# Attention matmuls of a hybrid encoder step: every score, turn and value product on the full 128 by 128 array

## The chip, the cores and the metric

The kernel runs on one core of one Trainium2 chip. It uses TensorE (matmuls, with a separate queue for weight loads), VectorE, ScalarE, GpSimd and SyncE, which starts most DMAs. The metric is the device time of one execution in microseconds, as the median of several runs. Before the change that is 2833.0 us (three runs, 2825.91 to 2838.61).

## The reference

Two layers of an encoder run over 512 prompt tokens and 64 sample tokens. Each layer has three sub-layers with a norm before and behind: token mixers, cross-attention into 256 memory tokens, and a squared-ReLU MLP. The mixers are latent attention (8 heads, keys of 64 + 32, values of 64), retention (4 heads), and band attention (8 heads of 64, with a learned bias). The part that matters here is the softmax attention of the two mixers with heads of 64:

```
s = einsum('bqhd,bkhd->bhqk', q, k) * scale (+ bias, or a mask)
p = softmax(s, axis=-1)
o = einsum('bhqk,bkhd->bqhd', p, v)      # v has 64 columns a head
```

The sample tokens attend to 256 cached keys and to their own 64. The memory attention has 4 heads of 128.

## The kernel before

Activations lie feature-major: 128 features on the partitions, all 576 tokens along the free axis. Weights stream in units of 128x1024 and are split into a rounded and a remainder part, so that a projection is three passes of float32r for each of 8 tiles of features, in two halves of 288 tokens (`project`, L332). A projection is called a job; there are two buffers for jobs in PSUM, which VectorE empties.

`attend` runs an attention stage on TensorE, ScalarE and VectorE, each with its own copy of the loop. An item is one head and one tile of 128 queries; there are five a head: four of the prompt, whose keys are the 128, 256, 384 and 512 up to there, and one of the sample tokens, with 320 keys (256 of the cache, 64 new). The scores of an item are issued two items ahead. The order of an item is:

- `scores` (L360): TensorE multiplies queries (stationary) with keys (moving), into one of two banks.
- `maxima` on VectorE: in the band stage first the scaling and the bias (L1024), then the row maximum (L1028).
- `exps` on ScalarE (L697), `normalise` on VectorE (L1036 to L1038).
- `turn` (L370): TensorE transposes the probabilities by tiles of 128 keys, with an identity as the moving operand.
- `copy_turned` on ScalarE (L705, L708): the turned tiles go to SBUF. The last tile of the sample item has 64 keys and gets a copy of its own.
- `weigh` (L381): TensorE multiplies value tiles (stationary) with the turned probabilities. For heads of 64 the stationary operand has 64 columns and the result goes to partitions 0 to 63 or 64 to 127, by the head's parity. For the sample item's third key tile only 64 rows are used.
- `round_output` on ScalarE (L716) and `split_output` on VectorE (L1045), which frees the output bank (`out_free`).

TensorE's order within step j of the loop is: scores of item j+2, weighing of item j-1, turning of item j, and then the projections that a plan puts there for the next head (latent, memory) or the next pair of heads (band). VectorE's order is: normalise item j, the plan's evictions, maxima of item j+2, split of item j-1. `PLAN_MLA` puts keys and values, queries, and the transposed values of the next head behind items of the current one. `PLAN_BAND` puts the projections for queries, keys and values of the next pair, and its values' transposes (L350), behind items 1, 3, 5 and 7 of ten.

In the band stage the queries and keys of a pair of heads share one tile: even head on partitions 0 to 63, odd head on 64 to 127. The scores use 64 rows of both. In the latent stage they use 100 rows (96 features and 4 for the mask). In the memory stage everything is 128 by 128.

`v_sb` holds two buffers of seven value tiles: 0 to 3 prompt, 4 and 5 cache, 6 the new sample tokens. Retention uses the same memory. `cs_sb` holds the cosine and sine tables of latent attention and retention; nothing uses it during the band and memory stages. `Q` is also the scratch for squares (`SQ`) and for retention.

Of the kernel before, what the change touches and what calls it, by code (L numbers as in the profile page):

```python
# [9 lines left out]
ALU = mybir.AluOpType  # L10
ACT = mybir.ActivationFunctionType
AX_X = mybir.AxisListType.X

P = 128
# [9 lines left out]
MASKS = 4  # L24
# [43 lines left out]

Q_TILES = [(i * P, (0, (i + 1) * P), [(j * P, P, j) for j in range(i + 1)]) for i in range(SEQ // P)]
Q_TILES.append((NT - P, (SEQ, DEC + PAST), [(DEC, P, 4), (DEC + P, P, 5), (0, DEC, 6)]))
MEM_TILES = [(i * P, (0, MEM), [(0, P, 0), (P, P, 1)]) for i in range(SEQ // P)]
MEM_TILES.append((NT - P, (MEM, MEM), [(0, P, 2), (P, P, 3)]))
# [52 lines left out]
def build(nc, x_in, mem_in, w_in, ckv_in, kpe_in, state_in, bandk_in, bandv_in, memk_in, memv_in,  # L127
          bias_in, gain_in, gain_x_in, const_in, rope_in, mask_in, y_out, ckv_out, kpe_out, retp_out, rets_out,
          bandk_out, bandv_out, memk_out, memv_out):
    with ExitStack() as ctx:  # L130
# [9 lines left out]
        def tiles(ap, k):  # L140
            return ap.rearrange("p (k n) -> p k n", k=k)
# [24 lines left out]
        TMP, Q, K = tiles(tmp_sb[:, :], 2), tiles(q_sb[:, :], 2), tiles(k_sb[:, :], 2)  # L166
        V = v_sb[:, :].rearrange("p (s t n) -> p s t n", s=2, t=7)
        PROB, BIAS = tiles(prob_sb[:, :], 3), tiles(bias_sb[:, :], 2)
        COS, SIN = cs_sb[:, 0:NT], cs_sb[:, NT:2 * NT]
        SQ = Q  # L170
        SUM = SQ[:, 0]
# [36 lines left out]
        def halves(ap):  # L208
            return ap.rearrange("p (b n) -> p b n", b=2)
# [43 lines left out]
        def _(pe):  # L253
# [15 lines left out]
            with pe.Fori(0, DEPTH) as l:  # L269
# [82 lines left out]

                def scores(i, head):
                    t0, (c, w), _ = head["tiles"][i]
                    r0, r1 = head["rows"]
                    it = n["item"]
                    s = it % 2

                    pe.wait_ge(exp_done, l * ITEMS + it + 1)
                    pe.matmul(score_ps[s][:, 0:w], Q[r0:r1, head["q"], t0:t0 + P], K[r0:r1, head["k"], c:c + w],  # L360
                              start=True, stop=True).then_inc(score_done, 1)
                    n["item"] += 1

                def turn(it, i, head):


                    pe.wait_ge(probs, l * ITEMS + it + 1)
                    pe.wait_ge(turned, l * ITEMS + it + 1)
                    for j, (c, w, _) in enumerate(head["tiles"][i][2]):
                        mm = pe.transpose(turn_ps[0:w, j * P:(j + 1) * P], PROB[:, it % 3, c:c + w], IDENT)  # L370
                    mm.then_inc(turn_done, 1)

                def weigh(it, i, head):

                    kts = head["tiles"][i][2]
                    pe.wait_ge(turned, l * ITEMS + it + 2)

                    pe.wait_ge(out_free, l * ITEMS + it + 1)
                    v0, v1, o0 = head["v"]
                    for j, (c, w, t) in enumerate(kts):  # L380
                        mm = pe.matmul(out_ps[o0:o0 + v1 - v0, 0:P], V[0:w, head["vs"], t, v0:v1],  # L381
                                       probT[0:w, j * P:(j + 1) * P], start=(j == 0), stop=(j == len(kts) - 1))
                    mm.then_inc(out_done, 1)

                def attend(heads, steps, when):
# [52 lines left out]
                def steps_mla(h):  # L438
                    s = []

                    def keys_values():
                        if h == 0:
                            wait_ready()
                        s.append(unit())
                        project(s[0], CR, CKV_HL, at_col=QR * P)
                        project(s[0], CR, CKV_HL, at_col=QR * P, pieces=[(0, PAST, NT)])

                    def queries():
                        if h == 0:
# [5 lines left out]
                    return [keys_values, queries,  # L455
                            lambda: turn_values(V_TOKENS + [(NT, P, 4), (NT + P, P, 5), (SEQ, DEC, 6)], but=1)]

                heads = [dict(q=h % 2, k=h % 2, rows=(0, QK + MASKS), tiles=Q_TILES, vs=h % 2,
                              v=(0, MLA_V, (h % 2) * MLA_V)) for h in range(MLA_HEADS)]
                attend(heads, steps_mla, PLAN_MLA)  # L460
                branch(last_output_split)

# [52 lines left out]

                def steps_band(p):
                    def values():
                        turn_values(V_TOKENS + [(SEQ, DEC, 6)])
                        pe.wait_ge(kv_loaded[p % 2], (l * 4 + p // 2 + 1) * 32)

                    return [lambda: project(unit(), KT, U_HL)] * 3 + [values]

                heads = [dict(q=h // 2 % 2, k=h // 2 % 2, rows=((h % 2) * 64, (h % 2) * 64 + 64),
                              tiles=Q_TILES, vs=h // 2 % 2, v=((h % 2) * 64, (h % 2) * 64 + 64, (h % 2) * 64))
                         for h in range(BAND_HEADS)]
                attend(heads, steps_band, PLAN_BAND)

# [12 lines left out]
                def steps_mem(h):  # L540
                    def query():
# [6 lines left out]
                heads = [dict(q=h % 2, k=h % 2, rows=(0, P), tiles=MEM_TILES, vs=h % 2, v=(0, P, 0))  # L548
                         for h in range(MEM_HEADS)]

                for step in steps_mem(0)[:MEM_FIRST]:
# [52 lines left out]
        def _(act):  # L604
# [40 lines left out]
            with act.Fori(0, DEPTH) as l:  # L645
# [55 lines left out]
                def copy_turned(it, i, head):  # L701
                    kts = head["tiles"][i][2]
                    act.wait_ge(turn_done, l * ITEMS + it + 1)
                    full = sum(k[1] == P for k in kts)
                    ins = act.activation(probT[:, 0:full * P], turn_ps[:, 0:full * P], ACT.Copy)  # L705
                    if full < len(kts):
                        w = kts[-1][1]
                        ins = act.activation(probT[0:w, full * P:(full + 1) * P],  # L708
                                             turn_ps[0:w, full * P:(full + 1) * P], ACT.Copy)
                    ins.then_inc(turned, 1)  # L710

                def round_output(it, i, head):
                    t0, t1, c0 = out_tokens(head["tiles"], i)
# [176 lines left out]
        def _(dve):  # L890
# [19 lines left out]
            with dve.Fori(0, DEPTH) as l:  # L910
# [9 lines left out]
                def free(ins):  # L920
                    ins.then_inc(job_free, 1)
# [199 lines left out]
                def steps_mla(h):  # L1121
# [27 lines left out]

                    def values():  # L1150
                        s = job()
                        v.tensor_copy(V[:, b, 0:4, 0:MLA_V], tiles(job_ps[s][:, 0:512], 4)[:, :, NOPE:P])
                        v.tensor_copy(V[:, b, 4:6, 0:MLA_V], tiles(job_ps[s][:, 512:768], 2)[:, :, NOPE:P])
                        free(v.tensor_copy(V[0:DEC, b, 6, 0:MLA_V], job_ps[s][0:DEC, 768 + NOPE:768 + P]))

                    return [keys_values, queries, values]

# [539 lines left out]
```

## Time and profile before

| | |
|---|---|
| median of the runs | 2833.0 us |
| profiled execution | 2829.17 us |
| its span | 2827.4 us, 46601 instructions |
| TensorE busy | 2606.2 us (92%), weight loads 2395.7 us (85%) |
| VectorE, ScalarE, GpSimd busy | 1443.0 (51%), 799.8 (28%), 826.7 (29%) |
| chain that ended last | TensorE 79%, VectorE 10%, its sequencer 6% |
| mean granted clock of TensorE | 0.959 |

The chain that ended last is followed back from the last instruction, at each step to what released it or to the instruction before it on its engine. A matmul's end is modelled and overlaps the next one's start, so the distance between starts tells what a pass costs, not its length. The latent stages run from 86.8 to 211.5 us in the first layer and from 1480.8 to 1605.6 in the second (first scores to last weighing), the band stages from 531.9 to 684.6 and from 1929.7 to 2080.2, the memory stages from 861.1 to 924.9 and from 2255.4 to 2321.7.

### The profile page before, as it was taken

Reading aid. Unit: us, or ns where it says so; the run is one execution under the profiler, and the core shown is the slowest. Engines: PE = TensorE matmul, PEld = TensorE weight load, DVE = VectorE, ACT = ScalarE, POOL = GpSimd, SP = SyncE. Lnnn points to the kernel's source line nnn. Section 1 sums busy time; section 2 is a strip of 40 time slices with the busy share of each in tenths; the row PEclk is TensorE's granted clock in tenths of the full one; section 3 lists DMA queues with packets and bytes.
Section 4 is the critical chain, followed back from the end, with each engine's and each line's share of the span. In section 5 each row is a group of like instructions: output and inputs, shape, how many; then the busy total and the mean of one; then the engine's idle time right before and its main releaser. Section 6 shows DMA issues by size and latency. Waiting matters only on the chain.

```text
span 2827.4 us, 46601 instructions
## 1 busy us (share of the span) xinstructions
PE 2606.2 (92%) x17836; PEld 2395.7 (85%) x17836; DVE 1443.0 (51%) x2226; ACT 799.8 (28%) x1460; POOL 826.7 (29%) x335
## 2 busy tenths in 40 slices
PE   8789999999989799999788999899999898999996
PEld 7669888877988799999676798797779787999995
DVE  4661464354564755346756515624445648353366
ACT  4342112234324311111324421223343343111112
POOL 3113223211333234434221132132223232343342
PEclk9999999999999999999899999899999999999998
DMA  4102112221223122222221121121222221222222
GB/s 140 38 23 93 60 47 85 71 75 61 83 71 94 46 82 84 88 82 84 61 82 31 48 83 49 43 92 61 81 76 80 68 89 48 83 85 83 82 83 78
DMA packets 65687, 204.73 MB, mean 72 GB/s; under 512 B 7936, under 2 KB 16000, under 8 KB 65360
## 3 DMA queue, kind: packets, MB, share of 16 engines
q10 hardware_dynamic: 47808, 174.08, 20.1%
q1 hardware_dynamic: 17680, 27.90, 3.0%
q8 instruction: 136, 2.23, 0.3%
q14 instruction: 63, 0.52, 0.1%
HBM read 190.93 MB, written 11.03 MB: 71 GB/s over the span
## 4 chain that ended last, share of the span: by engine, by line
PE 79%; DVE 10%; DVEq 6%; issue 2%; ACT 1%; DMA 0%; SPq 0%; ACTq 0%
PE job L332 65%; PE outp L381 5%; PE scores L360 3%; DVE rstd L974 3%; PE turn L370 2%; DVEq L1001 2%; PE scores L262 1%; DVEq L1037 1%; PE job L341 1%; DVE arena L965 1%; DVE rstd L982 1%; PE job L350 1%; ACT probT L705 1%; DVE x L1002 1%; DVEq L980 0%
## 5 line engine op out<-in xcount | busy, mean ns | idle before, releaser
L332 PE MATMUL job<-arena,w_hi 128*128 128x288 f32 (+1 forms) x9984 | 1775.5, 300 | 46.5 <-DVE q L1139 16.7
L332 PEld LDWEIGHTS job<-arena,w_hi 128*128 128x128 f32 x9984 | 1494.3, 192 | 67.6 <-issue 22.3
L593 POOL TENSOR_TENSOR w_lo<-raw,w_hi 128x1024 fp32r<-128x1024 f32 x331 | 826.5, 2497 | 1968.7 <-ACT w_hi L612 1968.7
L332 PE MATMUL job<-arena,w_lo 128*128 128x288 f32 (+1 forms) x4992 | 1087.6, 297 | 0.0
L332 PEld LDWEIGHTS job<-arena,w_lo 128*128 128x128 f32 x4992 | 818.8, 191 | 0.0
L612 ACT ACTIVATE w_hi<-raw 128x1024 fp32r<-128x1024 f32 x331 | 349.6, 1056 | 1072.0 <-PE job L332 904.7
L381 PEld LDWEIGHTS outp<-probT,v 128*64 128x64 f32 (+2 forms) x992 | 111.4, 149 | 141.5 <-issue 71.3
L948 DVE TENSOR_TENSOR tmp<-job,rstd 128x576 f32<-128x576 f32 x70 | 53.0, 758 | 329.9 <-PE job L332 325.5
L381 PE MATMUL outp<-probT,v 128*64 128x128 f32 (+2 forms) x992 | 160.8, 291 | 51.4 <-DVE arena L1045 38.7
L262 PE MATMUL scores<-q,const 128*128 128x288 f32 (+1 forms) x296 | 99.0, 473 | 69.6 <-ACT q L673 60.6
L360 PE MATMUL scores<-k,q 128*128 128x256 f32 (+10 forms) x400 | 148.5, 455 | 13.1 <-DVE k L1341 4.4
L937 DVE CAST arena<-tmp 128x576 fp32r<-128x576 f32 x64 | 151.6, 2368 | 4.7
L716 ACT ACTIVATE arena<-outp 64x128 fp32r<-64x128 f32 (+3 forms) x200 | 52.4, 262 | 312.9 <-PE outp L381 312.5
L262 PEld LDWEIGHTS scores<-q,const 128*128 128x128 f32 x296 | 60.8, 222 | 92.1 <-ACT q L673 69.2
L1387 DVE TENSOR_TENSOR m<-job,m 128x576 f32<-128x576 f32 x48 | 36.4, 758 | 194.3 <-PE job L332 194.3
L747 ACT ACTIVATE tmp<-tmp,gain 128x576 f32<-128x576 f32 x48 | 37.3, 778 | 256.4 <-DVE tmp L948 256.4
L1376 DVE SCALAR_TENSOR_TENSOR tmp<-job,rstd 128x576 f32<-128x576 f32 x64 | 48.5, 758 | 110.4 <-PE job L332 110.1
L943 DVE COPY m<-job 128x576 f32<-128x576 f32 x48 | 36.3, 756 | 124.9 <-PE job L332 124.9
L370 PE MATMUL turn<-const,prob 128*128 128x128 f32 (+1 forms) x496 | 99.7, 300 | 0.0
L974 DVE RECIPROCAL rstd<-rstd 128x576 f32<-128x576 f32 x22 | 82.5, 3752 | 31.3 <-ACT rstd L626 27.4
L705 ACT ACTIVATE probT<-turn 128x256 f32<-128x256 f32 (+3 forms) x200 | 83.6, 418 | 36.4 <-PE turn L370 32.3
L1045 DVE TENSOR_TENSOR arena<-outp,arena 64x128 fp32r<-64x128 f32 (+3 forms) x200 | 55.0, 275 | 65.3 <-ACT arena L716 60.8
(145 smaller groups left out, 1718.1 us busy)
## 6 DMA issues: line engine op xcount, KB each, us to landing
raw<-in_w ACTq DMA_DIRECT2D x332, 512.0 KB, 3.6
bias<-in_bias SPq DMA_DIRECT2D x16, 256.0 KB, 3.4
x<-in_x SPq DMA_DIRECT2D x4, 576.0 KB, 8.7
cs<-in_rope SPq DMA_DIRECT2D x4, 576.0 KB, 4.6
out_o_bandk<-k SPq DMA_DIRECT2D x8, 288.0 KB, 4.0
out_o_bandv<-tmp SPq DMA_DIRECT2D x8, 288.0 KB, 5.0
out_y<-x SPq DMA_DIRECT2D x1, 2304.0 KB, 6.9
bias<-in_mem SPq DMA_DIRECT2D x8, 256.0 KB, 3.5
```

The source lines that it names most:

```text
L262: mm = pe.matmul(scores_ps[:, po:po + nn], ONES, SQ[:, k % 2, so:so + nn], start=(k == 0), stop=(k == kt - 1))
L332: mm = pe.matmul(ps[0:m, po:po + nn], w[:, s, c:c + m], x[:, k, so:so + nn], start=(k == 0 and w is WHI and x is hl[0]), stop=(k == kt - 1 ...
L360: pe.matmul(score_ps[s][:, 0:w], Q[r0:r1, head["q"], t0:t0 + P], K[r0:r1, head["k"], c:c + w], start=True, stop=True).then_inc(score_done, 1)
L370: mm = pe.transpose(turn_ps[0:w, j * P:(j + 1) * P], PROB[:, it % 3, c:c + w], IDENT)
L381: mm = pe.matmul(out_ps[o0:o0 + v1 - v0, 0:P], V[0:w, head["vs"], t, v0:v1], probT[0:w, j * P:(j + 1) * P], start=(j == 0), stop=(j == len ...
L593: nc.gpsimd.tensor_tensor(WLO[:, u % RING, :], RAWS[:, u % RAW, :], WHI[:, u % RING, :].bitcast(F32), ALU.subtract).then_inc(lo_done, 1)
L612: act.activation(WHI[:, u % RING, :], RAWS[:, u % RAW, :], ACT.Copy).then_inc(hi_done, 1)
L705: ins = act.activation(probT[:, 0:full * P], turn_ps[:, 0:full * P], ACT.Copy)
L937: v.tensor_copy(hi, src)
L974: v.reciprocal(ap, ap)
L1001: dve.drain()
L1045: v.tensor_tensor(O_HL[1][o0:o1, ot, t0:t1], out_ps[o0:o1, c0:P], O_HL[0][o0:o1, ot, t0:t1].bitcast(F32), ALU.subtract).then_inc(out_free, 1)
```

## The change

- The weighing takes value tiles 128 columns wide. The result has 128 rows, of which a head of 64 uses the same 64 as before. In the latent stage the values of an even head lie in columns 0 to 63, of an odd head in columns 64 to 127, and the other columns hold whatever is there; in the band stage a tile holds both heads of a pair, as it did.
- Band queries get two tiles, one for even and one for odd heads, with zeros in the other head's 64 partitions. The scores multiply over all 128 rows. The even tile is `Q`, the odd one lies in `cs_sb`. VectorE scales the query projection in two operations, one for each, and sets the zeros once a layer, before the retention branch's output.
- The 64-long tail tile becomes 128 long: its transposes and its product cover 128 keys, where the probabilities of the extra 64 are multiplied with value rows that are zero. ScalarE copies all turned tiles in one instruction.
- At the start VectorE sets `v_sb` and `vT` to zero.

```diff
-Q_TILES = [(i * P, (0, (i + 1) * P), [(j * P, P, j) for j in range(i + 1)]) for i in range(SEQ // P)]
-Q_TILES.append((NT - P, (SEQ, DEC + PAST), [(DEC, P, 4), (DEC + P, P, 5), (0, DEC, 6)]))
+Q_TILES = [(i * P, (0, (i + 1) * P), [(j * P, j) for j in range(i + 1)]) for i in range(SEQ // P)]
+Q_TILES.append((NT - P, (SEQ, DEC + PAST), [(DEC, 4), (DEC + P, 5), (0, 6)]))
...
+        Q_EVEN, Q_ODD = Q, tiles(cs_sb[:, :], 2)
...  (scores, turn, weigh on TensorE)
-                    pe.matmul(score_ps[s][:, 0:w], Q[r0:r1, head["q"], t0:t0 + P], K[r0:r1, head["k"], c:c + w],
+                    pe.matmul(score_ps[s][:, 0:w], head["q"][0:rows, t0:t0 + P], K[0:rows, head["k"], c:c + w],
...
-                    for j, (c, w, _) in enumerate(head["tiles"][i][2]):
-                        mm = pe.transpose(turn_ps[0:w, j * P:(j + 1) * P], PROB[:, it % 3, c:c + w], IDENT)
+                    for j, (c, _) in enumerate(head["tiles"][i][2]):
+                        mm = pe.transpose(turn_ps[:, j * P:(j + 1) * P], PROB[:, it % 3, c:c + P], IDENT)
...
-                    v0, v1, o0 = head["v"]
-                    for j, (c, w, t) in enumerate(kts):
-                        mm = pe.matmul(out_ps[o0:o0 + v1 - v0, 0:P], V[0:w, head["vs"], t, v0:v1],
-                                       probT[0:w, j * P:(j + 1) * P], start=(j == 0), stop=(j == len(kts) - 1))
+                    for j, (_, t) in enumerate(kts):
+                        mm = pe.matmul(out_ps[:, 0:P], V[:, head["vs"], t, :], probT[:, j * P:(j + 1) * P],
+                                       start=(j == 0), stop=(j == len(kts) - 1))
...
-                heads = [dict(q=h // 2 % 2, k=h // 2 % 2, rows=((h % 2) * 64, (h % 2) * 64 + 64),
-                              tiles=Q_TILES, vs=h // 2 % 2, v=((h % 2) * 64, (h % 2) * 64 + 64, (h % 2) * 64))
+                heads = [dict(q=(Q_EVEN, Q_ODD)[h % 2][:, h // 2 % 2], k=h // 2 % 2, rows=P, tiles=Q_TILES, vs=h // 2 % 2)
...  (copy_turned on ScalarE)
-                    full = sum(k[1] == P for k in kts)
-                    ins = act.activation(probT[:, 0:full * P], turn_ps[:, 0:full * P], ACT.Copy)
-                    if full < len(kts):
-                        w = kts[-1][1]
-                        ins = act.activation(probT[0:w, full * P:(full + 1) * P],
-                                             turn_ps[0:w, full * P:(full + 1) * P], ACT.Copy)
-                    ins.then_inc(turned, 1)
+                    w = len(kts) * P
+                    act.activation(probT[:, 0:w], turn_ps[:, 0:w], ACT.Copy).then_inc(turned, 1)
...  (VectorE)
             v.memset(small[:, :], 0.0)
+            v.memset(v_sb[:, :], 0.0)
+            v.memset(vT, 0.0)
...
-                        v.tensor_copy(V[:, b, 0:4, 0:MLA_V], tiles(job_ps[s][:, 0:512], 4)[:, :, NOPE:P])
+                        o = b * MLA_V
+                        v.tensor_copy(V[:, b, 0:4, o:o + MLA_V], tiles(job_ps[s][:, 0:512], 4)[:, :, NOPE:P])
...
                 dve.sem_inc(phase_done, 1)
+                for b in range(2):
+                    v.memset(Q_EVEN[BAND_HD:P, b], 0.0)
+                    v.memset(Q_ODD[0:BAND_HD, b], 0.0)
                 branch(False, ahead=1)
...
+                    def queries():
+
+                        s = job()
+                        e = BAND_HD
+                        v.tensor_tensor(halves(Q_EVEN[0:e, b]), job_halves(s, 0, e), halves(rstd[0:e, :]), ALU.mult)
+                        free(v.tensor_tensor(halves(Q_ODD[e:P, b]), job_halves(s, e, P), halves(rstd[e:P, :]), ALU.mult))
...
-                    return [lambda: scale_job(Q[:, b]), keys, lambda: scale_job(vT[:, 0:NT]), values]
+                    return [queries, keys, lambda: scale_job(vT[:, 0:NT]), values]
```

## Rows read from the trace of the kernel before

**Rows 1.** Groups by shape, L381: count | busy us, mean ns | idle before
```profile
L381 PE MATMUL outp<-probT,v 128*64 128x128 f32 x768 | 122.4, 291 | 44.5 <-DVE arena L1045 33.1 <-ACT probT L705 8.4 <-ACT probT L708 2.5
...
L381 PE MATMUL outp<-probT,v 64*64 64x128 f32 x64 | 14.2, 304 | 0.0
```

**Rows 2.** Timeline, TensorE, latent stage: start us, us, engine, line, operation
```profile
156.37 1.02 PE L360 MATMUL scores<-k,q 100*128 100x512 f32 x2
157.32 0.43 PE L381 MATMUL outp<-probT,v 128*64 128x128 f32 x2
157.69 0.44 PE L370 MATMUL turn<-const,prob 128*128 128x128 f32 x2
157.96 0.70 PE L360 MATMUL scores<-k,q 100*128 100x320 f32 x2
```

**Rows 3.** Timeline, TensorE, memory stage
```profile
893.19 0.60 PE L360 MATMUL scores<-k,q 128*128 128x256 f32 x2
893.63 0.61 PE L381 MATMUL outp<-probT,v 128*128 128x128 f32 x4
894.07 0.38 PE L370 MATMUL turn<-const,prob 128*128 128x128 f32 x2
894.29 0.38 PE L350 MATMUL job<-const,tmp 128*128 128x128 f32 x2
...
895.02 0.68 PE L381 MATMUL outp<-probT,v 128*128 128x128 f32 x4
895.54 0.38 PE L370 MATMUL turn<-const,prob 128*128 128x128 f32 x2
```

**Rows 4.** Chain that ended last, one latent head: start us, us, what
```profile
140.68 0.75 DVE q L1134
...
144.22 0.62 PE outp L381 x4
...
147.78 0.60 ACT probT L705
...
154.15 0.13 PE job L332
```

**Rows 5.** Windows of two latent heads each: length, busy by engine, PEclk, DMA
```profile
122.43:154.15 31.72, 28.32 (x186) 21.61 (x186) 22.34 (x61) 14.37 (x44) 4.72 (x2) 1.00 0.12 34
154.15:188.99 34.84, 31.44 (x186) 24.34 (x186) 22.31 (x61) 14.37 (x44) 4.73 (x2) 0.90 0.11 31
```

**Rows 6.** Chain that ended last, one band pair
```profile
581.54 6.39 PE job L332 x48
...
602.29 0.13 PE job L332
```

**Rows 7.** Timeline, TensorE, band stage
```profile
576.18 1.06 PE L381 MATMUL outp<-probT,v 128*64 128x128 f32 x8 [0.93 <-DVE arena L1045]
...
579.69 1.12 PE L360 MATMUL scores<-k,q 64*128 64x512 f32 x2
580.74 0.43 PE L381 MATMUL outp<-probT,v 128*64 128x128 f32 x2
...
590.30 0.87 PE L381 MATMUL outp<-probT,v 128*64 128x128 f32 x6 [0.17 <-ACT probT L705]
```

**Rows 8.** Timeline, VectorE, band stage
```profile
580.31 0.35 DVE L1038 TENSOR_SCALAR prob<-prob,small 128x256 f32<-128x256 f32 x1
...
587.97 0.76 DVE L948 TENSOR_TENSOR q<-job,rstd 128x576 f32<-128x576 f32 x1 [4.92 <-PE job L332]
```

**Rows 9.** Timeline, VectorE, latent stage: a copy of 64 partitions
```profile
151.62 0.75 DVE L1144 COPY k<-job 64x576 f32<-64x576 f32 x1 [0.90 <-PE job L332]
```

**Rows 10.** Line 1169, a memset: count, ns min/median/max, first and last start
```profile
L1169 DVE MEMSET v<- x2: 165/165/165, 289.8 to 1683.9; 64x128 f32 x2
```

**Rows 11.** Timeline, end of the retention branch, first layer
```profile
446.31 0.76 DVE L948 TENSOR_TENSOR tmp<-job,rstd 128x576 f32<-128x576 f32 x1 [2.10 <-DMA out_o_rets<-k]
...
449.07 0.69 PE L332 MATMUL job<-arena,w_hi 128*128 128x288 f32 x4
```

More of the change, by code:

```diff
@@ L66 @@
 NCONST = _c
-Q_TILES = [(i * P, (0, (i + 1) * P), [(j * P, P, j) for j in range(i + 1)]) for i in range(SEQ // P)]
-Q_TILES.append((NT - P, (SEQ, DEC + PAST), [(DEC, P, 4), (DEC + P, P, 5), (0, DEC, 6)]))
-MEM_TILES = [(i * P, (0, MEM), [(0, P, 0), (P, P, 1)]) for i in range(SEQ // P)]
-MEM_TILES.append((NT - P, (MEM, MEM), [(0, P, 2), (P, P, 3)]))
+Q_TILES = [(i * P, (0, (i + 1) * P), [(j * P, j) for j in range(i + 1)]) for i in range(SEQ // P)]
+Q_TILES.append((NT - P, (SEQ, DEC + PAST), [(DEC, 4), (DEC + P, 5), (0, 6)]))
+MEM_TILES = [(i * P, (0, MEM), [(0, 0), (P, 1)]) for i in range(SEQ // P)]
+MEM_TILES.append((NT - P, (MEM, MEM), [(0, 2), (P, 3)]))
 NQ = len(Q_TILES)
@@ L354, in scores @@
                     t0, (c, w), _ = head["tiles"][i]
-                    r0, r1 = head["rows"]
+                    rows = head["rows"]
                     it = n["item"]
@@ L455, in steps_mla @@
                     return [keys_values, queries,
-                            lambda: turn_values(V_TOKENS + [(NT, P, 4), (NT + P, P, 5), (SEQ, DEC, 6)], but=1)]
-                heads = [dict(q=h % 2, k=h % 2, rows=(0, QK + MASKS), tiles=Q_TILES, vs=h % 2,
-                              v=(0, MLA_V, (h % 2) * MLA_V)) for h in range(MLA_HEADS)]
+                            lambda: turn_values(V_TOKENS + [(NT, P, 4), (NT + P, P, 5), (SEQ, P, 6)], but=1)]
+                heads = [dict(q=Q[:, h % 2], k=h % 2, rows=QK + MASKS, tiles=Q_TILES, vs=h % 2) for h in range(MLA_HEADS)]
                 attend(heads, steps_mla, PLAN_MLA)
@@ L517, in values @@
                     def values():
-                        turn_values(V_TOKENS + [(SEQ, DEC, 6)])
+                        turn_values(V_TOKENS + [(SEQ, P, 6)])
                         pe.wait_ge(kv_loaded[p % 2], (l * 4 + p // 2 + 1) * 32)
                     return [lambda: project(unit(), KT, U_HL)] * 3 + [values]
-                heads = [dict(q=h // 2 % 2, k=h // 2 % 2, rows=((h % 2) * 64, (h % 2) * 64 + 64),
-                              tiles=Q_TILES, vs=h // 2 % 2, v=((h % 2) * 64, (h % 2) * 64 + 64, (h % 2) * 64))
+                heads = [dict(q=(Q_EVEN, Q_ODD)[h % 2][:, h // 2 % 2], k=h // 2 % 2, rows=P, tiles=Q_TILES, vs=h // 2 % 2)
                          for h in range(BAND_HEADS)]
@@ L546, in steps_mem @@
                         lambda: turn_values([(0, P, 0), (P, P, 1)]), query]
-                heads = [dict(q=h % 2, k=h % 2, rows=(0, P), tiles=MEM_TILES, vs=h % 2, v=(0, P, 0))
+                heads = [dict(q=Q[:, h % 2], k=h % 2, rows=P, tiles=MEM_TILES, vs=h % 2)
                          for h in range(MEM_HEADS)]
@@ L1151, in values @@
                         s = job()
-                        v.tensor_copy(V[:, b, 0:4, 0:MLA_V], tiles(job_ps[s][:, 0:512], 4)[:, :, NOPE:P])
-                        v.tensor_copy(V[:, b, 4:6, 0:MLA_V], tiles(job_ps[s][:, 512:768], 2)[:, :, NOPE:P])
-                        free(v.tensor_copy(V[0:DEC, b, 6, 0:MLA_V], job_ps[s][0:DEC, 768 + NOPE:768 + P]))
+                        o = b * MLA_V
+                        v.tensor_copy(V[:, b, 0:4, o:o + MLA_V], tiles(job_ps[s][:, 0:512], 4)[:, :, NOPE:P])
+                        v.tensor_copy(V[:, b, 4:6, o:o + MLA_V], tiles(job_ps[s][:, 512:768], 2)[:, :, NOPE:P])
+                        free(v.tensor_copy(V[0:DEC, b, 6, o:o + MLA_V], job_ps[s][0:DEC, 768 + NOPE:768 + P]))
                     return [keys_values, queries, values]
```

## The prediction

> **What bounds the kernel now.** I read the page first: TensorE is busy for 92% of the 2827.4 us span and the chain that ended last is 79% TensorE, so time is mostly a matter of what TensorE issues and how densely. The diff touches three kinds of TensorE work, the scores (L360), the turning of probabilities (L370) and the weighing of values (L381), in the two stages of 8 heads (latent, then band). Of the weighing's passes 768 run as 128 rows by 64 columns, and 64 more as 64 by 64 (a float32 product is two passes) [rows 1]. Then I read TensorE's timeline where nothing waits, in the latent stage, beside the memory stage, whose heads are 128 wide and whose code the change leaves alone. There the difference stands in the starts. In the memory stage four weighing passes take 0.44 us from their first start to the first turn (893.63 to 894.07), 0.11 each, and two turns 0.22 (to 894.29) [rows 3]. In the latent stage two weighing passes take 0.37 to the first turn (157.32 to 157.69), and two turns then 0.27 (to 157.96) [rows 2]. So entering and leaving the narrow shape costs something that the full shape doesn't.
>
> **Price of one crossing.** Scores of 256 columns take 0.22 a pass (0.44 for two, 893.19 to 893.63) [rows 3]; 512 columns would take 0.43, two 0.86. In the latent stage two such passes take 0.95 before the weighing starts [rows 2]: 0.09 for going in. Two weighing passes would take 0.22 and take 0.37: 0.15 for the slower first step (about 0.05) and for going out (0.09). The first step after it, among the turns, has 0.27 for 0.22: 0.05. A crossing is 0.09 before and 0.05 behind; I count 0.145, since the rows are rounded to 0.01 and the two together gave 0.15 above. In the band stage scores read 64 rows: 512 columns take 1.05 [rows 7] where the latent stage has 0.95, so going into scores costs 0.09 + 0.10 = 0.19.
>
> The Trainium skill (TensorEngine Tiling (Array Packing), Key Properties) says that changing the tiling mode, not just the tile, drains TensorE. The 0.09 agrees with it in kind; the page gives no time. By its letter every matmul on part of the array would count, and the turns of 64 columns with them; my sum counts only crossings that cost something in the starts.
>
> **What goes, and what it is worth where.** All crossings: latent 80 items with one in, one out, and 16 more for the 64-long tail tile, 176 x 0.145 = 25.5 us; band 160 x 0.145 + 80 x 0.19 + 16 x 0.145 = 40.7 us. 66 us is the most, if TensorE set every step. It doesn't, so I go by stretches of one period.
>
> *Latent head, 15.86 us* (31.72 for two) [rows 5]. From 140.68 the chain is VectorE's (queries of the next head, the next maximum, the split of the last output), until the weighing may start at 144.22 [rows 4]. Crossings in that stretch are hidden and stay worth nothing. From 144.22 to 154.15 the chain is TensorE's but for ScalarE's copy of 0.60 (147.78). On it lie six crossings: into the weighing of 6 passes, out of it, out of the one of 8, into the one of 4 + 2, within it (128 to 64 rows), out of it: 0.87. Added: a weighing that starts out of a wait shows its load. In the memory stage four passes out of a wait take 0.52 (895.02 to 895.54) against 0.44 without one [rows 3], 0.08. A load of half the columns shows part of that already; between 0 and 0.08 I take 0.06, nearer to the row, for the weighing of 8, and 0.02 for passes a few ns longer. 0.79 a head. ScalarE's and VectorE's pieces in that stretch have over 0.3 us to spare before the step that needs them, so the next limit is not reached. Seven heads a layer carry this; the last has no projections in between, its weighings wait for ScalarE, and the tail's second copy goes: about 1.0. (7 x 0.79 + 1.0) x 2 layers = 13.0 us.
>
> *Band pair, about 40.7 us*, four stretches between its three projections.
> - After the value projection VectorE sets the pace (bias, maximum, normalising, copying values) to 576.18, where TensorE had waited 0.93 for its split [rows 7]; only the start of that line comes earlier, by 0.19 (shorter scores). +0.19.
> - 576.18 to 581.54 [rows 6, 7] holds eight crossings, 1.25 us, all on TensorE's chain. But VectorE is nearly as late: it normalised what the last turn needs until 580.66 [rows 8], and its work ahead of that stands without a gap, so it moves by 0.03 at most. The turn can start 0.05 behind it, at 580.68 instead of 581.10 (the 0.37 that two weighing passes take from 580.74, [rows 7, 2]): +0.42 of the 1.25.
> - Behind the query projection the change adds work: queries are scaled into two tiles. Now it is one operation of 0.76 at 587.97 [rows 8]; each of the two has 64 partitions and the same 576 columns, and a copy of 64x576 took 0.75 [rows 9]. Bounds: nothing (halves of 0.38) to 0.76 more; I take 0.72, by the copy and the overlap of neighbours. Queued behind it on VectorE are bias, maximum and split, which the weighing at 590.30 waits for; that weighing waited 0.17 for ScalarE already [rows 7]. It would start near 590.87, the next projection 0.46 later after what the crossings give back. -0.46.
> - Behind the key projection, to 602.29 [rows 6], seven crossings, 1.1 us; VectorE has slack, ScalarE's copy holds back 0.2. +0.89.
>
> 1.04 a pair, three pairs a layer; the last pair, without projections, half VectorE's, about 1.3; the prelude 0.3. (3.1 + 1.3 + 0.3) x 2 = 9.4 us.
>
> *Added elsewhere.* Four memsets of 64x576 a layer, on VectorE before the retention branch's output. A memset of 64x128 took 0.165 us [rows 10]; four cost 0.7 at least (no part of it by length) and 3.0 at most (all of it); I take 2.2, since most of such a price goes by length. Behind them waits the scaling at 446.31, which frees the buffer that TensorE takes at 449.07 [rows 11]: 446.31 + 2.2 + 0.76 = 449.27, 0.2 late here; I count the other layer at nothing, its spare time being of the same kind. Bounds 0 to 3.0 a layer; I take 0.2 in all. The two memsets at the start (2624 columns, 2 to 3.4 us by the same row) run while inputs are loading: nothing. The latent values' copies keep their sizes; the tail tile's longer turn and product cost no pass.
>
> *Sum*: 13.0 + 9.4 - 0.2 = 22 us. The profiled execution took 2829.2; it becomes 2807. The median of the runs lies 3.8 higher (2833.0), so I predict 2811.
>
> **Rivals**, their times against the runs' median.
> 1. *VectorE takes the place of the drains* in the latent stage too, and the band stage gives only its fourth stretches: half of the latent 13.0 and 5 of the band's 9.4 are left, 11 or 12. 2821. For it: VectorE is already the chain in three of the band's stretches. Against: in 144.22 to 154.15 no VectorE piece stands on the chain.
> 2. *The clock.* Two latent heads had a granted clock of 0.90 on average instead of 1.00 (parts of them at 1.2 in place of 2.4 GHz) and took 34.84 instead of 31.72 [rows 5], 1.56 each. TensorE's waits in VectorE's stretches get longer by what the crossings lose there. If nine more latent heads fell so, 14 us go back: 2825, no change that can be told. Against: what TensorE has to stream is the same or more.
> 3. *Slower: the full-width load.* 832 passes [rows 1] load 128 columns in place of 64. Exposed, it costs 0.06 (above); at every pass, on the chain, 832 x 0.06 = 50 us: 2833 - 22 + 50 = 2861. It decides from about 370 exposed loads on the chain on (22 / 0.06), and below that only eats the gain. Against: inside a row of passes the full shape keeps 0.11 [rows 3], so the load lies under the pass before; only starts out of a wait show it. The Trainium skill (TensorE: Matmul & The Clock Gate, LDWEIGHTS) has the load's time grow with the columns, P/1.2 ns, so about 53 ns more; by it, uncovered, 832 x 0.053 = 44 us would be added. The starts out of a wait agree with that size, the streams show it covered.
> 4. *It doesn't do what it says*: the 0.09 comes of the kind of work (product, then turn), not of its shape. Then only the added work is left, 0.2 for the memsets and 0.46 for the queries of three pairs in two layers: 2836. Against: the memory stage has the same order and no 0.09 [rows 3].
>
> **How the numbers follow.** Forecast 0.69, rival 1 0.12, rival 2 0.10, rival 3 0.05, rival 4 0.04. 0.5% (14 us) is about what a measurement of this kernel can tell from no change; faster by more means under 2819. That is the forecast but for its upper edge (0.65), and a part of the case of VectorE (0.05): 0.70. Same 0.25, slower 0.05 (the load alone). The range of 8 in 10: low end 2796, if VectorE's lines in the band stage give way and 37 of the 66 us come back; high end 2829, with the clock case and rival 1.
>
> **What would show it.** The weighing has one form, 128 by 128, and no idle time put down to issue; two weighing passes to the turn 0.22; latent heads near 15.1 us, band pairs near 39.7; latent stages shorter by 6 to 7 us, band stages by 4 to 5; VectorE the chain from 576 to 581. Wrong: a 0.09 that stays between weighing and turns, stages that keep their length, latent heads with a granted clock under 1 in most periods, or time lost outside the two stages.

## The result, and the profile after

| | before | after |
|---|---|---|
| median of 20 runs each | 2830.5 us (2812.2 to 2839.4) | 2810.1 us (2797.8 to 2827.2) |
| ratio after / before | | 0.9931, 95% interval 0.9914 to 0.9947 |
| profiled execution | 2829.17 us, span 2827.4 | 2799.22 us, span 2797.4 |
| mean granted clock | 0.959 | 0.963 |
| latent stage, layers 1 and 2 | 124.67, 124.76 | 123.35, 118.90 |
| of it at half clock (1.2 GHz) | 10.2, 10.2 | 20.5, 10.2 |
| band stage | 152.74, 150.45 | 144.42, 144.24 |
| of it at half clock | 18.7, 11.4 | 6.8, 6.8 |

About 20 us less, 0.7%. The page of the kernel after (busy time by engine; the chain by engine; the weighing's group):

```profile
PE 2556.0 (91%) x17836; PEld 2407.1 (86%) x17836; DVE 1453.8 (52%) x2244; ACT 799.2 (29%) x1428; POOL 827.6 (30%) x335
...
PE 77%; DVE 11%; DVEq 7%; issue 3%; ACT 1%; DMA 0%; SPq 0%; ACTq 0%
...
L381 PE MATMUL outp<-probT,v 128*128 128x128 f32 x992 | 157.8, 291 | 71.8 <-DVE arena L1040 59.9
```

The two narrow groups of [rows 1] have become one, 128 by 128, with as many passes as all forms had together. Most of its idle time stands beside VectorE (L1040, the split of the last output, 59.9 of 71.8 us), as it did before (33.1 of 44.5 in the larger narrow group). So a crossing doesn't show as idle time, before or after; it shows in the starts, below. The chain has less of TensorE and more of VectorE.

TensorE's timeline in the latent stage of the kernel after, where nothing waits (start us, length, engine and line, operation):

```profile
158.22 1.02 PE L361 MATMUL scores<-k,q 100*128 100x512 f32 x2
159.08 0.38 PE L381 MATMUL outp<-probT,v 128*128 128x128 f32 x2
159.30 0.38 PE L371 MATMUL turn<-const,prob 128*128 128x128 f32 x2
159.52 0.70 PE L361 MATMUL scores<-k,q 100*128 100x320 f32 x2
```

This answers to [rows 2]. Two weighing passes to the turn take 0.22 where they took 0.37, the two turns 0.22 for 0.27, the scores 0.86 for 0.95. These are the steps of the memory stage in [rows 3].

The same view at the weighing that VectorE holds back, in the kernel after and then before:

```profile
126.12 0.70 PE L361 MATMUL scores<-k,q 100*128 100x320 f32 x2
128.55 0.68 PE L381 MATMUL outp<-probT,v 128*128 128x128 f32 x4 [1.73 <-DVE arena L1040]
```

```profile
144.22 0.62 PE L381 MATMUL outp<-probT,v 128*64 128x128 f32 x4 [1.45 <-DVE arena L1045]
```

The wait has grown from 1.45 to 1.73 us. What the crossings lost in VectorE's stretch (0.29 in the steps above), TensorE now spends waiting. Two heads of the kernel after as windows (length, then busy time and count of TensorE, its loads, VectorE, ScalarE and GpSimd, granted clock, DMA share, GB/s):

```profile
109.72:124.82 15.10, 13.10 (x95) 11.36 (x93) 11.52 (x30) 7.27 (x21) 2.36 (x1) 1.00 0.11 36
124.82:141.44 16.62, 14.64 (x94) 13.01 (x93) 10.72 (x30) 7.09 (x21) 2.36 (x1) 0.90 0.11 33
```

At full clock a pair of neighbouring heads takes 14.97 + 15.10 us, where two took 31.72 in [rows 5]. A head with a stretch at half clock takes 16.6 to 16.8.

The chain of the kernel after through one band pair (start, length, what; "DVEq" is VectorE's sequencer):

```profile
573.34 0.39 DVE prob L1033
573.72 0.46 DVEq L1021
...
577.71 0.44 PE turn L371 x2
578.15 6.40 PE job L333 x48
...
584.58 0.75 DVE q L1306
585.33 0.78 DVEq L1021
...
587.59 0.91 PE outp L381 x6
...
588.93 6.38 PE job L333 x48
595.31 0.43 PE scores L361 x2
...
598.59 1.47 PE job L333 x11
```

From 573.34 on VectorE is the chain up to the last two turns (577.71). That stretch, 573.21 to 578.15, takes 4.94 where it took 5.36. Behind the query projection (584.55) two VectorE pieces of about 0.75 stand in the chain (584.58, and 585.33, the second scaling, shown as its sequencer), and 4.38 us pass to the next projection instead of 3.83. Behind the key projection nothing but TensorE is left: 3.28 (595.31 to 598.59) instead of 4.15. TensorE's timeline of that pair:

```profile
573.21 1.13 PE L381 MATMUL outp<-probT,v 128*128 128x128 f32 x8 [1.20 <-DVE arena L1040]
574.17 0.49 PE L371 MATMUL turn<-const,prob 128*128 128x128 f32 x3
...
576.12 1.02 PE L361 MATMUL scores<-k,q 128*128 128x512 f32 x2
577.18 0.46 PE L381 MATMUL outp<-probT,v 128*128 128x128 f32 x2
...
587.59 0.91 PE L381 MATMUL outp<-probT,v 128*128 128x128 f32 x6 [1.51 <-DVE arena L1040]
```

Scores of 512 columns take 1.06 to the weighing (576.12 to 577.18), but that weighing is one that VectorE is late for: its split ends at 577.03. The 8 passes at 573.21 take 0.96 from a wait to the turn.

### The profile page after: what moved, and what is told of

It is laid out like the page before. It is cut to its first block, busy times and chain, and to the rows that moved or that the text cites. A ratio compares the mean times of both kernels' runs of the same rounds, so it can differ in the third digit from the quotient of the medians.

```text
span 2797.4 us, 46587 instructions
## 1 busy us (share of the span) xinstructions
PE 2556.0 (91%) x17836; PEld 2407.1 (86%) x17836; DVE 1453.8 (52%) x2244; ACT 799.2 (29%) x1428; POOL 827.6 (30%) x335
## 4 chain that ended last, share of the span: by engine, by line
PE 77%; DVE 11%; DVEq 7%; issue 3%; ACT 1%; DMA 0%; SPq 0%; ACTq 0%
PE job L333 65%; PE outp L381 4%; DVE rstd L969 3%; PE scores L361 2%; DVEq L996 2%; DVEq L1032 2%; PE turn L371 1%; PE scores L263 1%; PE job L342 1%; DVE arena L960 1%; PE job L351 1%; DVE rstd L977 1%; DVE prob L1019 1%; DVEq L1021 1%; ACT probT L703 1%
## 5 line engine op out<-in xcount | busy, mean ns | idle before, releaser
L333 PE MATMUL job<-arena,w_hi 128*128 128x288 f32 (+1 forms) x9984 | 1770.6, 299 | 47.6 <-DVE q L1134 16.8
L381 PEld LDWEIGHTS outp<-probT,v 128*128 128x128 f32 x992 | 135.2, 196 | 139.3 <-ACT probT L703 75.7
L381 PE MATMUL outp<-probT,v 128*128 128x128 f32 x992 | 157.8, 291 | 71.8 <-DVE arena L1040 59.9
L361 PE MATMUL scores<-k,q 128*128 128x256 f32 (+9 forms) x320 | 115.9, 449 | 12.1 <-DVE k L1347 4.4
L371 PE MATMUL turn<-const,prob 128*128 128x128 f32 x496 | 91.6, 283 | 1.0 <-DVE prob L1033 0.6
L1033 DVE TENSOR_SCALAR prob<-prob,small 128x256 f32<-128x256 f32 (+4 forms) x200 | 76.0, 380 | 17.1 <-issue 1.8
```

What stands on the lines that cost most here:

```text
L333: mm = pe.matmul(ps[0:m, po:po + nn], w[:, s, c:c + m], x[:, k, so:so + nn], start=(k == 0 and w is WHI and x is hl[0]), stop=(k == kt - 1 ...
L361: pe.matmul(score_ps[s][:, 0:w], head["q"][0:rows, t0:t0 + P], K[0:rows, head["k"], c:c + w], start=True, stop=True).then_inc(score_done, 1)
L371: mm = pe.transpose(turn_ps[:, j * P:(j + 1) * P], PROB[:, it % 3, c:c + P], IDENT)
L381: mm = pe.matmul(out_ps[:, 0:P], V[:, head["vs"], t, :], probT[:, j * P:(j + 1) * P], start=(j == 0), stop=(j == len(kts) - 1))
L1033: v.tensor_scalar(PROB[:, it % 3, 0:w], PROB[:, it % 3, 0:w], small[:, s * 4 + 3:s * 4 + 4], None, ALU.mult).then_inc(probs, 1)
```

## The experiments

A pair is one period of the band stage, at full clock and with the next pair's projections in it. "Low heads" counts the latent periods (one head to the next), of 14 in a profile, with more than 1 us at half clock. The last kernel has a single execution and no ratio.

| kernel | ratio to before (95%) | pair, us | full-clock latent heads, us | low heads |
|---|---|---|---|---|
| before | 1 | 40.66 | 15.83, 15.89 | 5 |
| after | 0.9931 (0.9914 to 0.9947) | 39.73 | 14.97, 15.10 | 7 |
| after, repeated | 0.9928 (0.9903 to 0.9953) | 39.73 | 14.97, 15.12 | 8 |
| narrow values in the memory stage of before | 1.0005 (0.998 to 1.003) | 40.65 | 15.85, 15.88 | 3 |
| after, band scores on 64 rows | 0.9966 (0.9948 to 0.9985) | 39.78 | 14.98, 15.09 | 7 |
| before, band scores on 128 rows | 0.9971 (0.9953 to 0.9989) | 40.44 | 15.83, 15.89 | 2 |
| after, second scaling deferred | 0.9940 (0.9918 to 0.9962) | 38.81 | 14.97, 15.09 | 9 |
| the same, repeated | 0.9929 (0.9903 to 0.9955) | 38.83 | 14.98, 15.10 | 9 |
| and band values copied by ScalarE | 0.9895 (0.9871 to 0.9920) | 37.90 | 14.97, 15.12 | 8 |
| after, filled wait | 0.9887 (0.9860 to 0.9913) | 39.74 | 14.98, 15.11 | 0 |
| all three | **0.9845 (0.9823 to 0.9868)** | 37.91 | 14.98, 15.11 | 0 |
| before, later queries (one run) | | 40.66 | 16.20, 16.25 | 7 |

### Narrow values in the memory stage

The shape alone, in a stage that the change leaves alone. Half of the memory heads' output is left out.

```diff
-heads = [dict(q=h % 2, k=h % 2, rows=(0, P), tiles=MEM_TILES, vs=h % 2, v=(0, P, 0))
+heads = [dict(q=h % 2, k=h % 2, rows=(0, P), tiles=MEM_TILES, vs=h % 2, v=(0, 64, 0))
```

> The kernel before, but the memory attention, which was 128 by 128, weighs only 64 of its 128 value columns (the other half of its output is left out). Theory (the shape's change costs, 0.09 us before and 0.05 behind each crossing): four weighing passes to the first turn take 0.58 us instead of 0.44, two turns then 0.27 instead of 0.22, scores to weighing 0.09 more; 40 items gain two crossings each, 11.6 us at most, about 6 on the chain; the memory stages get longer by 2 to 5 us each, nothing else changes. Rival (the cost comes of the order product then turn, or of waits, not of the shape): 0.44 and 0.22 stay and the memory stages keep their length.

TensorE's timeline in its memory stage:

```profile
897.91 0.60 PE L360 MATMUL scores<-k,q 128*128 128x256 f32 x2
898.43 0.65 PE L381 MATMUL outp<-probT,v 128*64 128x128 f32 x4
899.01 0.44 PE L370 MATMUL turn<-const,prob 128*128 128x128 f32 x2
899.29 0.38 PE L350 MATMUL job<-const,tmp 128*128 128x128 f32 x2
899.51 0.60 PE L360 MATMUL scores<-k,q 128*128 128x256 f32 x2
```

The 64-column passes bring with them what [rows 2] has: scores to weighing 0.52 instead of 0.44 in [rows 3], four passes to the turn 0.58 instead of 0.44, the turns 0.28 instead of 0.22. A head takes 19.51 us instead of 18.98. So the price belongs to the shape, not to the kind of work; rival 4 falls. In total 8 heads lose 0.53 each, which no ratio of this kernel can show, and it doesn't. The Trainium skill (TensorEngine Tiling (Array Packing), Key Properties) says that a change of tiling mode drains TensorE. The trace agrees for the products, not for the turns of 64 columns that the kernel before had, each of which starts 0.11 us behind the turn before it, like a full one.

### Band scores on 64 rows again

```diff
-heads = [dict(q=(Q_EVEN, Q_ODD)[h % 2][:, h // 2 % 2], k=h // 2 % 2, rows=P, ...
+heads = [dict(q=Q[:, h // 2 % 2], k=h // 2 % 2, rows=(h % 2 * 64, h % 2 * 64 + 64), ...
...  (VectorE: the zeros go too)
-    return [queries, keys, lambda: scale_job(vT[:, 0:NT]), values]
+    return [lambda: scale_job(Q[:, b]), keys, lambda: scale_job(vT[:, 0:NT]), values]
```

> The changed kernel with the band scores put back on 64 rows: one query tile, one scaling, no zeros set for it; weighing, turns and tail stay full. Theory (each stretch goes by what sets it, TensorE or VectorE): latent heads stay at 15.06 us. A band pair: behind the value projection +0.19, the stretch that VectorE sets 0 to +0.1, behind the query projection -0.73 (the second scaling goes), behind the key projection +0.62 (two crossings into scores at 0.19, two out of them at 0.145): +0.2 a pair, 39.9 instead of 39.7, 1 to 2 us for the program over the changed kernel. Rival (every crossing counts in full): 80 x (0.19 + 0.145) less 6 x 0.75, 22 us over the changed kernel, so as slow as before.

TensorE's timeline in its band stage:

```profile
575.52 1.12 PE L361 MATMUL scores<-k,q 64*128 64x512 f32 x2
576.57 0.49 PE L381 MATMUL outp<-probT,v 128*128 128x128 f32 x2
```

1.05 for two passes of 512 columns on 64 rows, as in [rows 7], and the pair is as long as with the padding: 39.78 against 39.73. The zero-padded queries, as they stand, buy nothing in a pair; what they save in crossings, the second scaling spends. The ratio is nearer to 1 than that of the kernel after (0.9966 against 0.9931, about 10 us); no part of the pairs explains that. The band stages, 145.49 and 146.67 us against 144.94 in the mean of four with the padding, hold 2 us of it; the rest stays open.

### Band scores on 128 rows alone

The reverse: the kernel before with the two query tiles and `rows=(0, P)` in the band stage, values and tail tile as they were.

> The kernel before with the band scores alone padded to 128 rows (two query tiles, two scalings, zeros set once a layer); weighing and tail stay narrow. Theory: latent heads stay at 15.87 us. A band pair: behind the value projection -0.19, next stretch -0.38, behind the query projection +0.65, behind the key projection -0.38: -0.3, 40.4 instead of 40.66; the program 2 us under the kernel before, not to be told from it. Rival (the padding carries the gain of the band stage): pairs near 39.7, band stages 5 us shorter each.

Pairs of 40.44, as expected, and latent heads as before. The pairs' 0.22 times 6 explain 1.3 us of the 8 that the ratio gives (0.0029 of 2833). The band stages, 146.88 and 148.80 us against 150.96 in the mean of four with 64-row scores, are 6 us shorter together, so the padding takes more off the stage than off its pairs: half clock was 6.8 and 11.4 us there, 13.2 in the mean of the four. And this profile has little half clock in its latent stages (2 low heads against 5), so its ratio says less of the edit than its pairs.

### The second scaling deferred

The odd queries' scaling moves into the step of the next job, ahead of the keys' scaling, where VectorE waits for the key projection and has time to spare.

```diff
 def queries():
     ...
-    free(v.tensor_tensor(halves(Q_ODD[e:P, b]), job_halves(s, e, P), halves(rstd[e:P, :]), ALU.mult))
 def keys():
+    s = (n["job"] - 1) % 2
+    e = BAND_HD
+    free(v.tensor_tensor(halves(Q_ODD[e:P, b]), job_halves(s, e, P), halves(rstd[e:P, :]), ALU.mult))
```

> The changed kernel, but VectorE scales the odd heads' queries one step later, in the time in which it waits for the key projection; the same operations. Theory (the second scaling stands on the chain only because bias, maximum and split are queued behind it): the stretch behind the query projection falls from 4.38 to about 3.63 us, pairs from 39.7 to 39.0, 6 pairs: 4.5 us under the changed kernel, ratio to the kernel before about 0.9915. Rival (the stretch is set by ScalarE's copy or by the turns anyway): 4.38 falls by 0.2 at most and the pairs stay at 39.6.

The chain behind its query projection:

```profile
583.32 0.75 DVE q L1306
584.07 0.13 DVEq L1021
...
585.43 0.91 PE outp L381 x6
...
586.77 6.38 PE job L333 x48
```

One scaling in the chain, and 3.47 us from the projection's end (583.30) to the next one (586.77) instead of 4.38. The pair falls by 0.92 to 38.81. The whole 0.76 of the second scaling had been on the path, and a little more. But the ratio didn't tell this kernel from the kernel after. Both were run again, side by side:

> The changed kernel once more, beside the next two on the same chip. Theory: ratio to the kernel before 0.993 again; latent heads 15.06 us where the granted clock is full, band pairs 39.7 and 40.1. The feed-forward stages, which the change leaves alone, run at one of two paces of a pass, 130.0 or 133.3 ns, whichever kernel it is; 10 us a stage.

> The kernel with the odd heads' queries scaled one step later, once more. Theory: pairs of 38.8 and 39.2 us, so 5.5 us under the changed kernel where the feed-forward stages run at the same paces; the timed ratio 0.991 to 0.994. Rival (what the band pairs give back goes elsewhere, as the first timing, 0.994, may say): the stages outside the band stage get longer by as much.

The pairs repeat to 0.03 us, and the ratios still don't part (0.9928 and 0.9929). 0.92 x 6 is 5.5 us, and the intervals are 14 us wide; but the traces show where the 5.5 went. The end of the first band stage as windows, from the weighing behind the last scores of 512 columns to the last weighing, in the kernel after and then with the scaling deferred:

```profile
666.90:675.95 9.05, 5.87 (x41) 4.54 (x40) 5.59 (x16) 4.81 (x14) 0.00 (x0) 1.00 0.00 0
663.81:675.51 11.70, 8.53 (x40) 6.87 (x39) 5.58 (x16) 4.81 (x14) 0.00 (x0) 0.70 0.00 0
```

VectorE and ScalarE do the same work in both, but TensorE's granted clock is 0.70, and the stretch is 2.65 us longer. All four band stages of the two deferred profiles end so, and one of four in the kernel after. The deferred stages take 144.31 to 144.56 us, as long as the three of the kernel after that end at full clock (144.22 to 144.42). So the rival of the repetition is right in that what the pairs give back goes elsewhere: into the last head of the same stage. TensorE's waits there are the same in both (1.0, 0.69 and 0.58 us), so why its clock falls in one of them stays open.

### The band values copied by ScalarE

Beside the deferred scaling, ScalarE takes the two copies of the band values out of PSUM.

```diff
 def values():    # ScalarE
+    n["job"] += 1
+    act.wait_ge(job_done, l * JOBS + n["job"] + 1)
+    s = (n["job"] - 1) % 2
+    act.activation(V[:, p % 2, 0:4, :], tiles(job_ps[s][:, 0:512], 4), ACT.Copy)
+    act.activation(V[0:DEC, p % 2, 6, :], job_ps[s][0:DEC, 768:768 + P], ACT.Copy).then_inc(job_free, 1)
...
 def values():    # VectorE
-    s = job()
-    v.tensor_copy(V[:, b, 0:4, :], tiles(job_ps[s][:, 0:512], 4))
-    free(v.tensor_copy(V[0:DEC, b, 6, :], job_ps[s][0:DEC, 768:768 + P]))
+    n["job"] += 1
```

> As the kernel with the deferred queries, and ScalarE instead of VectorE copies the band values out of PSUM (0.69 + 0.27 us a pair). Theory (VectorE sets the stretch behind the value projection): 0.9 us less a pair, pairs near 38.0 and 38.3, 10 to 11 us under the changed kernel at equal paces, ratio 0.989. Rival (TensorE or ScalarE is next within 0.3 us there): pairs near 38.5 and 38.9.

ScalarE's timeline in its band stage (the copies stand ahead of the exponentials of the sample item):

```profile
571.02 0.60 ACT L817 ACTIVATE v<-job 128x512 f32<-128x512 f32 x1
571.52 0.26 ACT L818 ACTIVATE v<-job 64x128 f32<-64x128 f32 x1
```

Pairs of 37.90, another 0.91 less. With VectorE in three of the four stretches, what is taken from it shows at once. The band stages take 138.80 and 139.06 us, 5.5 less than with the deferred scaling alone: half of that is the pairs', the other half comes from the last head, which here stays at full clock.

### The wait filled

In the profiles with narrow latent values 10 of 42 latent periods were low (the expectation below says 9 and four kernels; it was 10 and three), in those with wide ones 48 of 84. Inside the heads, each fall came within 1.5 us behind the wait for VectorE's query work. So four passes are put there whose result is overwritten before it is read.

```diff
...  (in the latent stage's call: fill=True)
+if fill and j % NQ == 2 and j + NQ < len(flat):
+    pe.wait_ge(job_free, l * JOBS + at["job"] + n["job"] + 1)
+    for _ in range(2):
+        pe.matmul(job_ps[n["job"] % 2][:, 0:3 * P], IDENT, const[:, 0:3 * P], start=True, stop=True)
 if j:
     weigh(base + j - 1, flat[j - 1][1], flat[j - 1][0])
```

> The kernel after, with two products of the identity and 384 constant columns (four passes, about 1.3 us, overwritten before anything reads them) put on TensorE in the latent stage of heads 0 to 6, in front of the weighing that waits for VectorE's query work. In the profiles of the four kernels with narrow latent values, 9 of 42 latent head periods had a stretch at half clock; in those of the six profiles with wide ones, 48 of 84. What stands ahead of each is the same wait of TensorE, 1.44 us in the narrow form and 1.73 in the wide one. Theory (the longer wait brings the clock down): the wait falls to about 0.4, at most 2 of 14 periods fall to half clock, their length at full clock stays 15.05, a latent stage takes 116 to 118 us instead of 122.7 on average, the execution some 10 us less than the kernel after, ratio to before about 0.989. Rival 1 (the clock falls because the passes themselves are denser, or by chance): 6 to 9 of 14 periods stay low, the time stays within 2 us of the kernel after or grows, ratio 0.993. Rival 2 (the added passes are themselves on the chain): full-clock periods get longer than 15.1.

TensorE's timeline at the place, and two heads as windows:

```profile
123.28 0.70 PE L361 MATMUL scores<-k,q 100*128 100x320 f32 x2
123.82 1.45 PE L409 MATMUL job<-const 128*128 128x384 f32 x4
125.72 0.68 PE L381 MATMUL outp<-probT,v 128*128 128x128 f32 x4 [0.44 <-DVE arena L1045]
```

```profile
106.88:121.98 15.10, 14.39 (x99) 12.11 (x97) 11.52 (x30) 7.25 (x21) 2.36 (x1) 1.00 0.11 36
121.98:136.96 14.98, 14.29 (x98) 12.12 (x97) 10.63 (x30) 7.08 (x21) 2.36 (x1) 1.00 0.10 37
```

The wait is 0.44 instead of 1.73, the heads keep their 14.98 and 15.10, the granted clock is 1.00, and no head of 14 is low. The latent stages take 114.09 and 116.90 us; the second has 6.8 us at half clock ahead of its first period, where nothing is filled. Together that is 14 us less than two wide stages in the mean (122.65 each), and the ratio goes from 0.9928 to 0.9887, 12 us. Joined with the two edits before:

> The kernel with the odd queries' scaling moved behind the key projection and the band values copied by ScalarE, with the same four added passes in the latent heads. Theory: band pairs stay at 37.9 and the latent stages take 116 to 118 us instead of 123.35; 2803 less about 10 is 2793, ratio to before about 0.986. Rival (the clock does not go by that wait): 2803, ratio 0.9895.

2790.3 us in the median of five runs, 43 less than before, with pairs of 37.91 and no low head: the best version of the study.

### Later queries in the kernel before

The other direction: the wait is made longer and every pass stays narrow.

```diff
+v.memset(RTMP[0:NOPE, 0:256], 0.0)
 dve.drain()
 free(v.tensor_tensor(Q[NOPE:QK, b], Q[NOPE:QK, b], RTMP[NOPE:QK, :], ALU.add))
```

> The kernel before with one thing added: a memset of 64x256 on VectorE inside the latent queries' work, about 0.3 us by the 0.165 us of 64x128, so that TensorE's wait there becomes as long as the wide form's (1.73 us) while every TensorE pass stays narrow. Theory (the length of the wait decides): full-clock latent heads take 16.1 instead of 15.86, and about 4 of 7 a layer, 7 to 9 of 14, have a stretch at half clock instead of 1 to 2 of 7. Rival (the wide, denser passes bring the clock down): 2 to 4 of 14, as in the kernels with narrow values.

```profile
129.94 0.75 PE L381 MATMUL outp<-probT,v 128*64 128x128 f32 x4 [1.80 <-DVE arena L1045]
```

```profile
109.59:125.84 16.25, 14.18 (x94) 10.80 (x93) 11.79 (x31) 7.19 (x22) 2.36 (x1) 1.00 0.12 34
125.84:143.62 17.78, 15.73 (x94) 12.13 (x93) 11.08 (x31) 7.18 (x22) 2.36 (x1) 0.90 0.08 31
```

The wait is 1.80 in front of 128x64 passes, and 7 of 14 periods are low, in the second row with a granted clock of 0.90. The three profiles with narrow values and the shorter wait had 5, 3 and 2. So a longer wait brings about as many falls without the denser passes as with them; but one execution with 7, beside the 5 of the kernel before, suggests this and doesn't show it. What is shown is the other direction: wide passes with the wait filled, 0 of 28 periods in two kernels against 48 of 84. Which of the equal waits brings a fall stays open. The Trainium skill (TensorE: Matmul & The Clock Gate, Part 1: The HAM clock gate (the "warmup" mystery)) says that the throttled state is the default and that activity releases it; the filled wait, with a granted clock of 1.00 behind it, agrees.

## Why the prediction was right, and where it was not

**Price of a crossing.** Right. From scores of 512 columns to the weighing 0.43 a pass instead of 0.52, from the last weighing pass to the turn 0.11 instead of 0.20 (medians over the stage): 0.09 going in, 0.09 coming out. Scores on 64 rows keep 1.05.

**Latent head.** Predicted 0.79, measured 0.82 (15.86 to the mean of 14.97 and 15.10). At full clock throughout, a narrow latent stage took 120.04 us (the memory experiment, layer 2) and a wide one 114.09 (the filled wait, layer 1): 5.95 a layer, where 6.5 was predicted. The end of the stage gave 1.0 where 1.8 had been counted (0.79 for the seventh head and 1.0 for the last).

**The clock.** Here the prediction went wrong, though its total didn't. Rival 2 was set at 0.10, and its counter-argument was that TensorE streams as much or more. The runs show that this doesn't help. The falls go by the wait in VectorE's stretch: the same rival had said it would lengthen, it went from 1.45 to 1.73, and with the wait filled no head is low. Low heads rose from 10 of 42 to 48 of 84, from 3.3 to 8 an execution, at 1.6 us each 7.5 us, 3.7 a layer. Another 1.4 a layer goes to half clock in the stage's first microseconds, ahead of the first period. By stage, over nine profiles (all but the last three), the latent stage is 123.37 us in the mean of 6 narrow ones and 122.65 of 12 wide ones: 0.7 a layer is left of 5.95. "Latent heads under 1 in most periods" was named as a sign against the forecast, and it came.

**Band pair.** Predicted 40.66 to 39.62, measured 39.73. By stretches: behind the value projection -0.20 (predicted -0.19), to the query projection -0.42 (-0.42), behind it +0.55 (+0.46), behind the key projection -0.87 (-0.89). The deferred scaling shows the third term, the 64-row scores that the padding's gain and cost cancel. Two stages with nearly the same half clock, 150.25 with 11.2 us of it (the memory experiment) and 144.24 with 6.8 (after), differ by 6.0; with half of the 4.4 us taken off, as an estimate, 3.8 is the change's, where 4.7 was predicted. A part of what is missing is seen in the trace: where the last pair begins, VectorE idles 0.43 ahead of a normalising, which costs 0.33 and is put down to no releaser.

**What made the total right.** The band stage gained more than its crossings: from 150.96 in the mean of four (before and the memory experiment) to 144.94 of four (after and its repetition), 6.0 a layer, as less of it ran at half clock (13.2 us in the mean, then 8.5). The stretch from there to the memory stage fell by 1.7, from 175.55 to 173.82, in the same profiles, with no edit in it. 2 x (0.7 + 6.0 + 1.7) is 17 us; the ratio says 15 to 24. So the sum of 22 held because what the latent stages gave to the clock came back about as much elsewhere. The prediction had counted neither, so that part of its agreement is luck. The other profiles say that the return goes in part with the kernel: the half clock around the start of the band stage lasts 10.2 us in 4 of 8 layers with 64-row scores and at most 6.8 in the 16 with padded ones; the one at its end comes in 7 of 8 layers with narrow values and in 6 of 16 with wide ones, 4 of the 6 with the deferred scaling alone. What in the edits does it stays open.

**Memsets.** Predicted 2.2 us; they take 4 x 0.54 = 2.15 us a layer, 2.6 with the gaps between them. Behind them TensorE waits 0.29 us for its buffer in the first layer and 0.39 in the second, where the kernel before had no wait: 0.7 in all instead of 0.2, too little to see in a ratio.

**Rivals 1 and 3.** VectorE took over where the prediction had put it and not in the latent stretch that was said to be free of it. The full-width load stays covered: inside a row of passes 0.11 each; 8 passes out of a wait take 0.96, that is 0.08 more than without one.

## What to carry to other kernels

A matmul on part of the array costs at its borders; count the borders on the chain, not all of them. Where a faster engine only waits longer for another, look at its clock: the wait can take back most of the gain, and here a few harmless passes in it gave back some 12 us. Test an edit by the periods that it touches, since the median of a kernel with 15 us of spread can't tell 5; then look at the whole stage, since the last head can lose at half clock what the periods gained.

## What was not expected of the hardware

The feed-forward stages, which no kernel here changes, run at one of two paces. TensorE's timeline in the first layer, in the kernel after and in the one with 64-row scores:

```profile
1014.34 0.68 PE L333 MATMUL job<-arena,w_hi 128*128 128x288 f32 x4
...
1015.12 0.68 PE L333 MATMUL job<-arena,w_hi 128*128 128x288 f32 x4
...
1015.89 0.68 PE L333 MATMUL job<-arena,w_hi 128*128 128x288 f32 x4
```

```profile
1014.32 0.69 PE L333 MATMUL job<-arena,w_hi 128*128 128x288 f32 x4
...
1015.12 0.69 PE L333 MATMUL job<-arena,w_hi 128*128 128x288 f32 x4
...
1015.92 0.69 PE L333 MATMUL job<-arena,w_hi 128*128 128x288 f32 x4
```

Six passes take 0.78 and 0.77 in the one and 0.80 in the other; over 240 passes it is 130.0 and 133.3 ns a pass, at a granted clock of 1.00 in both. One pace holds for a whole stage. Of the 24 such stages in twelve profiles four ran at 130.0: the first layer's in before and after, the second layer's in the memory experiment and with 64-row scores. A stage has some 3000 passes, so the pace is worth about 10 us. This fits the profiled execution of the kernel after, which at 2799.2 us lies 11 below its median, and its repetition with both stages at 133.3 took 2819.5. Of the other three executions with a stage at 130.0, two lie 9 and 16 us below their medians, that of the kernel before only 1. The other executions have no trace, so that the pace makes the spread of the runs is argued and not shown; what sets it stays open.
